# A hybrid decoder step on one core: the input stage asks for x earlier, holds three late weight slabs, and starts eight gathers of cached indexer keys

## The reference

```python
mod = (jax.nn.silu(c) @ w_ada + b_ada)[:, None, :]            # 6 x 1024 columns: shift, scale, gate, twice
h   = rms_norm(xp, g_attn_norm[l]) * (1 + ca_p) + sa_p        # 1024 prompt rows and 8 sample rows
p   = h @ w_in                                                # 1024 x 2536, split among the head groups
keys_idx = jnp.concatenate([past_rows(cache_idx, pages), ki]) # per request: 64 pages of 128 cached keys
r     = relu(einsum('qhd,sd->qhs', q_idx, keys_idx) * IDX_DIM ** -0.5)
score = einsum('qh,qhs->qs', w_idx, r)                        # its 256 largest choose the keys of sparse attention
```

## Time and profile before

| | us |
|---|---|
| median of 3 runs (lowest to highest) | 2939.24 (2938.51 to 2941.61) |
| the profiled execution | 2946.87 |
| its span, first to last instruction | 2945.1 |
| PE busy in the span | 2564.5 (87%) |
| DVE, ACT, POOL busy | 1515.4, 1103.8, 373.3 |
| DMA, mean over the span | 174 GB/s |

### The profile page before, as it was taken

One profiled execution on the slowest core, in us unless ns is written; L12 is line 12 of the kernel. 1 busy time (PEld: TensorE's weight loads), 2 busy tenths in 40 slices (PEclk: granted clock), 3 DMA queues, 4 the chain that ended last, 5 costly groups with the idle time before them and its releaser, 6 DMA issues. The chain is left out here.

```text
span 2945.1 us, 44078 instructions
## 1 busy us (share of the span) xinstructions
PE 2564.5 (87%) x14550; PEld 1470.6 (50%) x14550; DVE 1515.4 (51%) x3765; ACT 1103.8 (37%) x2376; POOL 373.3 (13%) x419
## 2 busy tenths in 40 slices
PE   4998996859989899895889969798999899999977
PEld 1443443538778687784566624344333333333332
DVE  1456544468878877784898664584111111111126
ACT  1223212449879578783655501221111111111110
POOL 0000001011011010101232131052000010000025
PEclk7999997969999899996999989898999999999988
DMA  8022158332145021206110084216989898897867
GB/s 326 17 83 84 36 177 290 142 105 72 54 151 207 5 104 36 86 6 175 36 34 18 9 272 128 101 36 238 398 315 396 327 346 327 321 372 274 317 249 276
DMA packets 252353, 511.70 MB, mean 174 GB/s; under 512 B 24138, under 2 KB 102156, under 8 KB 244761
## 3 DMA queue, kind: packets, MB, share of 16 engines
q1 hardware_dynamic: 196300, 311.88, 30.7%
q0 software_dynamic: 28640, 127.09, 11.7%
q10 hardware_dynamic: 27252, 70.69, 6.3%
HBM read 631.86 MB, written 86.93 MB: 244 GB/s over the span
## 5 line engine op out<-in xcount | busy, mean ns | idle before, releaser
L2906 PE MATMUL routed_ex_pG<-dispatch_exWG,routed_ex_XT 128*64 128x512 f32 x2048 | 459.9, 605 | 32.8 <-DMA dispatch_exWG<-in_w_e_gu 27.8
L2030 DVE TENSOR_REDUCE ssqc<-SQ 128x8 f32<-128x512 f32 x516 | 346.2, 683 | 127.1 <-ACT SQ L1833 113.6
L1744 PE MATMUL eK<-dWkv,LT 128*128 128x256 f32 x1032 | 318.8, 392 | 12.2 <-ACT SQ L1833 11.7
L1747 PE MATMUL eK<-WA,LT 128*128 128x272 f32 x1032 | 329.3, 401 | 0.0
L2906 PEld LDWEIGHTS routed_ex_pG<-dispatch_exWG,routed_ex_XT 128*64 128x64 f32 x2048 | 149.1, 140 | 338.1 <-issue 337.8
L1833 ACT ACTIVATE SQ<-eK 128x512 f32<-128x512 f32 x516 | 291.9, 602 | 59.1 <-PE eK L1747 43.5
L2997 DVE TENSOR_TENSOR routed_ex_sg<-routed_ex_sg,routed_ex_pG 128x256 f32<-128x256 f32 x64 | 27.0, 421 | 555.3 <-ACT routed_ex_sg L2954 555.3
L556 PE MATMUL in_pp<-ada_Win,in_hT 128*128 128x512 f32 (+1 forms) x640 | 280.9, 597 | 9.8 <-ACT in_pr L454 9.8
L2925 PE MATMUL routed_ex_pY<-routed_ex_WD,routed_ex_AT 128*64 128x512 f32 x1024 | 233.8, 598 | 0.9 <-DMA routed_ex_WD<-in_w_e_down 0.9
L1747 PEld LDWEIGHTS eK<-WA,LT 128*128 128x128 f32 x1032 | 202.1, 196 | 29.5 <-DVE numc L2029 0.2
L1744 PEld LDWEIGHTS eK<-dWkv,LT 128*128 128x128 f32 x1032 | 191.2, 197 | 48.2 <-ACT SQ L1833 16.9
(11 more groups left out here) (550 smaller groups left out, 3715.2 us busy)
## 6 DMA issues: line engine op xcount, KB each, us to landing
dispatch_exWG<-in_w_e_gu SPq DMA_DIRECT2D x256, 1024.0 KB
routed_ex_WD<-in_w_e_down SPq DMA_DIRECT2D x132, 1024.0 KB, 19.2
s_yblk<-routed_ex_Y ACTq DMA_DIRECT2D x64, 512.0 KB
ada_Win<-in_w_ada ACTq DMA_DIRECT2D x8, 2048.0 KB, 11.1
s_yblk<-zrows SPq DMA_DIRECT2D x15, 1024.0 KB
ada_Wada<-in_w_ada SPq DMA_DIRECT2D x8, 1024.0 KB, 16.2
ada_Win<-in_w_in ACTq DMA_DIRECT2D x4, 2048.0 KB, 11.5
dispatch_exWG<-in_w_e_gu SPq DMA_DIRECT2D x4, 2048.0 KB
```

The costliest lines, as they stand in the source:

```text
L1744: pe.matmul(pK[kn % 3][:, 512 + z:512 + z + HK], key, Wkv[:, 4:8, 0:NOPE], start=True, stop=True)
L1747: pe.matmul(pK[kn % 3][:, z:z + HK + 16], key, WA[:, pr, :], start=True, stop=True).then_inc(s_KN, 1)
L2030: dve.tensor_reduce(ssqc[cg % 2][:, n - 1 - tau, :], SQ[kn % 4].rearrange("p (h d) -> p h d", h=H), AX.X, ALU.add).then_inc(s_red, 1)
L2906: m = pe.matmul(pG[u][r, :], XT[u][:, k, r], WG[2 * u + v][:, k, :], start=(k == 0), stop=(k == KD - 1))
```

## The change

Five edits:

1. SP asks for x0 after four of the eight slabs in `stage_ada`, not after all eight.
2. The page table is read at the start of `stage_in`, behind the second tile of x, and DVE makes the row numbers in step 1 there. `stage_index` no longer does either.
3. ACT asks for late slab 1 together with slab 2, one `take` later, and first waits until the stores of tile 6 have landed. Slab 7 is asked for after the last tile's second-last group of `roots`, not with slabs 4 to 6. PE multiplies three slabs in step 8 and five in step 9, where it was four and four.
4. POOL gathers the first eight blocks of keys within `stage_in`, once `s_lm` says that all eight slabs have been multiplied, into columns 0 to 2047 of `Win`. Blocks 4 to 7 each wait until the block four before has landed. `Win` is kept until `stage_index` ends and takes the place of the `KI` buffers.
5. In `stage_index` PE transposes the first block before it turns the queries. The modulation's sum is written to `sq` instead of `pr`.

```diff
+NQI, NKI = 4, 8
+def cached_keys(T):
+    return T["cache_idx_k"][0].rearrange("n (j s) d -> (n j) (s d)", j=NQI)
+def key_slab(G, k):
+    return G["Win"][:, k, 0:32 * IDX]
@@ stage_ada, SP
             for k in range(KD):
+                if k == 4:
+                    sp.dma_start(G["x0"][:, :], T["x_prompt"][0, 0:P, :]).then_inc(G["s_x0"], 16)
                 sp.dma_start(W[k][:, :], T["w_ada"][0, k * P:(k + 1) * P, 0:2048]).then_inc(s_w[k], 16)
...
-            sp.dma_start(G["x0"][:, :], T["x_prompt"][0, 0:P, :]).then_inc(G["s_x0"], 16)
@@ stage_in, SP
             load(1)
+            sp.dma_start(G["pages"][:, :], T["page_table"].rearrange("(a b) p -> (b p) a", b=2), allow_slow_non_contiguous=True).then_inc(s_pg, 16)
...
-                    sp.dma_start(T["mod"][:, a:a + 512], pr[(NTT - 3) % 3][32 * j:32 * j + NC9, late(2 + b)]).then_inc(G["s_tail"], 16)
+                    sp.dma_start(T["mod"][:, a:a + 512], sq[32 * j:32 * j + NC9, late(b)]).then_inc(G["s_tail"], 16)
+        @block.gpsimd
+        def _(pool):
+            pool.wait_ge(s_idx, 1)
+            pool.wait_ge(s_lm, KD)
+            for g in range(NKI):
+                if g >= 4:
+                    pool.wait_ge(G["s_ki"][g - 4], 16)
+                pool.indirect_dma_start(out=key_slab(G, g), out_offset=None, in_=cached_keys(T),
+                                        in_offset=bass.IndirectOffsetOnAxis(ap=G["didx"][:, g // NQI, g % NQI:g % NQI + 1], axis=0)).then_inc(G["s_ki"][g], 16)
@@ stage_in, ACT
                 elif step == NTT:
-                    for k in range(4, KD):
+                    for k in range(4, KD - 1):
                         act.wait_ge(s_lm, k - 3)
                         late_weights(k)
...
                 take(step, 1)
-                if step == NTT - 1:
-                    late_weights(1)
...
                     roots(t, (4, 5))
+                    if t == NTT - 1:
+                        act.wait_ge(s_lm, 4)
+                        late_weights(KD - 1)
                 take(step, 2)
                 if step == NTT - 1:
+                    act.wait_ge(s_rd, NTT - 2)
+                    late_weights(1)
                     late_weights(2)
@@ stage_in, PE
                 if step == NTT - 1:
-                    for k in range(4):
+                    for k in range(3):
                         late_modulation(k)
                 elif step == NTT:
-                    for k in range(4, KD):
+                    for k in range(3, KD):
                         late_modulation(k)
@@ stage_in, DVE
+                if step == 1:
+                    dve.wait_ge(s_pg, 16)
+                    link(dve.tensor_copy(G["pagef"][:, :], G["pages"][:, :]))
...
+                    dve.sem_inc(s_idx, 1)
@@ stage_index, POOL
-            pool.wait_ge(s_idx, 1)
-            for g in range(NG):
-                if g >= NKI:
-                    pool.wait_ge(s_T, 4 * (g - NKI + 1))
-                if g >= 4:
-                    pool.wait_ge(s_k[(g - 4) % NKI], 16 * ((g - 4) // NKI + 1))
...
+            for g in range(NKI, NG):
+                pool.wait_ge(s_T, 4 * (g - NKI + 1))
+                pool.wait_ge(s_k[(g - 4) % NKI], 16 * ((g - 4) // NKI + 1))
...
@@ stage_index, PE
             turns(0)
+            queries()
             pe.wait_ge(s_qb, 1)
```

More of the change, by code:

```diff
@@ L171, in build @@
         G["pagef"] = sb("pagef", [P, NS // 2])
+        G["didx"] = sb("didx", [P, NS // 2, NQI], I32)
         G["SD"] = sb("SD", [P, NS // 2, PAGE + 1])
@@ L182, in build @@
                 G["s_tail"] = nc.alloc_semaphore("in_last_stores")
+                G["s_ki"] = [nc.alloc_semaphore(f"keys{i}") for i in range(NKI)]
                 G["s_win"] = [nc.alloc_semaphore(f"win{g}") for g in range(len(in_cols()))]
@@ L348, in stage_in @@
     late = lambda q: slice(512 * q, 512 * q + 512)
+    s_pg, s_idx = sem("in_pages"), sem("in_key_rows")
+    idxf = sb("idxf", [P, NS // 2, NQI])
     NROOT = 7
@@ L741, in _ @@
             for b in range(2):
[L742 to L743 removed]
+                dve.tensor_tensor(sq[:, late(b)], pp[b][:, :], pr[(NTT - 3) % 3][:, late(b)], ALU.add).then_inc(s_lmod, 1)
 def stage_prompt(nc, T, G, sem, sb, ps):
@@ L1319, in stage_index @@
     c, pages, pagef, SD = G["c"], G["pages"], G["pagef"], G["SD"]
-    NP2, NQ, NKI = NS // 2, 4, 8
+    NP2, NQ = NS // 2, NQI
     NG = NP2 * NQ
-    KI = [sb(f"KI{i}", [P, 32, IDX]) for i in range(NKI)]
+    KI = [key_slab(G, i).rearrange("p (s d) -> p s d", d=IDX) for i in range(NKI)]
     qr = sb("dqr", [NS, H, 2, IDX])
@@ L1332, in stage_index @@
     RL = [sb(f"RL{i}", [P, 512]) for i in range(2)]
-    idx, idxf = sb("didx", [P, NP2, NQ], I32), sb("didxf", [P, NP2, NQ])
+    idx = G["didx"]
     pT, pS, pZ = [ps(f"dT{i}") for i in range(4)], [ps("dS0"), ps("dS1")], [ps("dZ0"), ps("dZ1")]
-    s_pg, s_q, s_idx, s_qt, s_qb, s_T, s_evd, s_eva, s_S, s_R, s_v, s_z, s_wx, s_wc, s_ws, s_sd = (
-        sem("di_" + n) for n in ("pg", "q", "idx", "qt", "qb", "T", "evd", "eva", "S", "R", "v", "z", "wx", "wc", "ws", "sd"))
-    s_k = [sem(f"di_k{i}") for i in range(NKI)]
-    idx_rows = T["cache_idx_k"][0].rearrange("n (j s) d -> (n j) (s d)", j=NQ)
+    s_q, s_qt, s_qb, s_T, s_evd, s_eva, s_S, s_R, s_v, s_z, s_wx, s_wc, s_ws, s_sd = (
+        sem("di_" + n) for n in ("q", "qt", "qb", "T", "evd", "eva", "S", "R", "v", "z", "wx", "wc", "ws", "sd"))
+    s_k = G["s_ki"]
     fresh = T["o11"].rearrange("l b s d -> (l b s) d")
@@ L1352, in _ @@
         def _(pool):
-            pool.wait_ge(s_idx, 1)
-            for g in range(NG):
-                if g >= NKI:
-                    pool.wait_ge(s_T, 4 * (g - NKI + 1))
-                if g >= 4:
-                    pool.wait_ge(s_k[(g - 4) % NKI], 16 * ((g - 4) // NKI + 1))
-                pool.indirect_dma_start(out=KI[g % NKI][:, :, :].rearrange("p s d -> p (s d)"), out_offset=None, in_=idx_rows,
+            for g in range(NKI, NG):
+                pool.wait_ge(s_T, 4 * (g - NKI + 1))
+                pool.wait_ge(s_k[(g - 4) % NKI], 16 * ((g - 4) // NKI + 1))
+                pool.indirect_dma_start(out=key_slab(G, g % NKI), out_offset=None, in_=cached_keys(T),
                                         in_offset=bass.IndirectOffsetOnAxis(ap=idx[:, g // NQ, g % NQ:g % NQ + 1], axis=0)).then_inc(s_k[g % NKI], 16)
@@ L1363, in _, with queries @@
         def _(pe):
-            pe.wait_ge(s_q, 64)
-            for h in range(H):
-                m = pe.transpose(pZ[0][:, h * NS:(h + 1) * NS], qr[:, h, :, :].rearrange("b a d -> b (a d)"), c("ident")[0:NS, 0:NS])
-            m.then_inc(s_qt, 1)
-            pe.wait_ge(s_wx, 1)
-            pe.matmul(pZ[1][:, 0:NP2], WX[:, :, :].rearrange("b r h -> b (r h)"), c("pair_of")[0:NS, :], start=True, stop=True)
-            pe.matmul(pZ[1][:, NP2:2 * NP2], c("last_of")[0:NS, :], fpr[:, :], start=True, stop=True).then_inc(s_wc, 1)
+            def queries():
+                pe.wait_ge(s_q, 64)
+                for h in range(H):
+                    m = pe.transpose(pZ[0][:, h * NS:(h + 1) * NS], qr[:, h, :, :].rearrange("b a d -> b (a d)"), c("ident")[0:NS, 0:NS])
+                m.then_inc(s_qt, 1)
+                pe.wait_ge(s_wx, 1)
+                pe.matmul(pZ[1][:, 0:NP2], WX[:, :, :].rearrange("b r h -> b (r h)"), c("pair_of")[0:NS, :], start=True, stop=True)
+                pe.matmul(pZ[1][:, NP2:2 * NP2], c("last_of")[0:NS, :], fpr[:, :], start=True, stop=True).then_inc(s_wc, 1)
             def turns(g):
```

14 lines of the change are left out of this document (4 added, 10 removed).

## The result

| | before | after |
|---|---|---|
| median, us (lowest to highest, 5 runs each) | 2941.61 (2938.51 to 2944.34) | 2959.20 (2957.11 to 2966.79) |
| ratio, 95% interval | | 1.0069 (1.0052 to 1.0085) |
| the profiled execution, us | 2946.87 | 2958.91 |
| SP's first request of the index stage, us | 490.02 | 508.90 |
| PE's first product there, us | 504.72 | 520.99 |

What follows compares the result with a forecast made beforehand. It took DMA to bound the input loading, then a chain from ACT's slab requests through PE to SP's stores; PE bounds the index loop. 0 + 0 + 16.8 - 1.8 = 15.0 us on the median 2939.24 gave 2954.2, range 2940 to 2959.

Steps and rivals of the forecast that it cites:

- Edit 1, 0: Start of the input stage: asking for x0 earlier costs 0, as DMA engines are full and bytes the same.
- Edit 2, 0: Input stage: the early page table and row numbers cost 0, 1 us at most if the third tile is delayed.
- Edit 3, slabs: Input stage's end: ACT free 4.7 us sooner, slab 7 landed at 471.9, PE at the last tile 1.7 us later.
- Edit 4, gathers: Input stage's end: SP's stores move 52 pieces a microsecond under gathers; with the slabs, the stage ends 16.8 us later.
- Edit 5, -1.8: Index stage: first product 12.9 us after its start instead of 14.7, a gain of 1.8 us, bounds 1 and 3.4.
- Fair share: Rival, input stage's end: SP's stores get their fair share beside the gathers, total 2939.8 to 2944.7 us; chance 0.21.
- The slabs pay: Rival, input stage's end: the slabs pay and the gathers are hidden, faster, 2933.9 us; chance 0.07.
- More than forecast: Rival: stores slow the gathers, or queries land 3 us or more late behind queued stores, 2959 to 2965 us; chance 0.08.

Runs made afterwards that it cites:

- x0_only: Kernel before with edit 1 alone (x0 asked for after four slabs instead of eight); ratio to before 1.0008 (0.9998 to 1.0019).
- numbers_ready: Kernel before with edit 2, all gathers at the index stage's start, PE's order as before; ratio to before 0.9999 (0.9990 to 1.0008).
- slabs_only: Kernel before with edit 3 alone (three late slabs, then five, slab 7 asked for later); ratio to before 1.0005 (0.9996 to 1.0014).
- keys_first: numbers_ready with one difference: PE transposes the first keys ahead of the queries; ratio to before 1.0013 (1.0003 to 1.0024).
- x0_undone: Kernel after without edit 1 (x0 again asked for behind all eight slabs); ratio to before 1.0059 (1.0046 to 1.0073).
- gathers_held: Kernel after with POOL's eight early gathers held until SP has issued its last input-stage request; ratio to before 1.0109 (1.0093 to 1.0125).
- loads_ahead: Kernel before with page table and small loads asked for before the last tile's stores, s_mod before transposed stores, gathers at index stage's start; ratio 0.9986 (0.9976 to 0.9995).
- mods_first: Kernel after with SP's eight s_mod requests ahead of the last tile's transposed stores; ratio to before 1.0062 (1.0049 to 1.0075).
- gathers_only: Kernel after without edits 1 and 3, eight gathers still in the input stage; ratio to before 1.0050 (1.0035 to 1.0066).
- two_early: Kernel before with edit 2 and PE's new order, two gathers in the input stage, the rest in the index stage; ratio 1.0008 (0.9999 to 1.0017).
- mods_pages: mods_ahead with the page table read behind the last tile's plain stores and gathers at the index stage's start; ratio to before 1.0011 (1.0002 to 1.0021).
- mods_pages_act: mods_pages with the four loads of queries, wi and fresh key asked for by ACT instead of SP; ratio to before 1.0007 (0.9996 to 1.0018).
- mods_ahead: Kernel before with the eight s_mod stores asked for ahead of the last tile's transposed stores; ratio to before 0.9996 (0.9987 to 1.0005).

## Why the prediction was right or wrong

The direction and the main mechanism were right: slower, by stores that stand behind gathers. What failed are the two terms that I had put at nothing, edits 1 and 2. The time was 5.0 us too low (2959.2 against 2954.2), just above the stated range. 2.4 of these are the base, 2941.61 with two more runs instead of 2939.24. 1.3 are in the trace up to the first product (16.3 against 15.0) and the last 1.3 between the trace and the medians. Up to the last stage's barrier the trace is 17.1 us later, close to the medians' 17.6.

The start of the index stage came 18.9 us later, not 16.8. These 2.1 are a sum of misses with both signs: edit 1 +1.0, edit 2 +1.8, the slabs +0.4 (1.6 against 1.2), the gathers -1.2 (14.4 against the 15.6 that are left of 16.8 without the slabs' 1.2). That the forecast came near is in part luck: the gathers' term and edit 5 took back 2.0 of what the others had missed. By its steps:

- *Edit 1, 0: wrong, the step that failed in kind.* "The DMA engines are full and the bytes are the same" left out the time between ACT's request and its data. 2.5 us ran at 249 GB/s instead of 391. DVE starts 1.66 us later in after and 1.3 in x0_only; 1.0 is left at the index stage there. I had even named the price, 1.3 us, and called it covered.
- *Edit 2, 0: wrong.* In numbers_ready all of edit 2 and the new place of the sum stand at +1.8 where the index stage starts. 1.4 of it come back in the other kernels that have them, 0.4 of it at 182 us and 1.0 in SP's last requests; the page table's pieces ahead of the third tile, the one cost that I had looked at, is neither. Which of the moved things makes the 1.4 is open.
- *Edit 3, slabs: right in kind, mis-sized.* ACT was forecast free 4.7 us sooner; it was 3.8 in slabs_only and 2.5 in after. Slab 7 was forecast landed at 471.9; PE got it at 474.57 (473.64 in slabs_only), outside my 470 to 473. The "about 1 to be reported" in that sum was my guess, and no run shows it: from q10's last piece to PE's matmul it was 0.5 us, 474.1 to 474.57 in after and 467.0 to 467.47 in before. The wait of 8 us was 7.32, the sixteen matmuls 3.55 against 3.8. So PE reached the last tile at 478.05, not 475.7. At the full clock it won 0.86 back in its first eight transposes and 1.4 in all, where I had put 0.5, and SP asked at 483.59, not 482.1.
- *Edit 4, gathers: right, a little too large.* 53 pieces a microsecond against 52. They started 3.4 us later than forecast (479.09), for slab 7 and 1.0 us between PE's last matmul and POOL. POOL asked until 494.96, not 491. The two long requests waited 8.83 and, in the first `s_mod`, 10.50 us, 19.3 together (15 to 20 forecast). That `s_mod` was taken at 504.63, when 1916 of SP's pieces had moved since the request for `qmT`; I had counted on the 2285 of before. SP ended at 507.41 against 505.4. What I had missed is POOL's drain. It was hidden in after, and so my reading that "POOL's program ends at about 491" set a bound was 14 us off: it ended at 505.2.
- *Edit 5, -1.8: right, a little small.* 2.6 measured. The value hangs on the keys being there; without them the same order costs 4.5 us (keys_first).
- *Rivals.* Fair share is refuted by q1's 9.0%. "The slabs pay" asked for slab 7 within 5.4 us of its request; it took 10. "More than forecast" named 2959 to 2965, and the median lies at its lower edge, but not by its mechanism: the queries landed 2.5 us after the request (508.90 to 511.39), so nothing queued there, and the gathers were through near 503 us, no later against the forecast's 499.7 than they had started. The drain that waits for the gathers stood in no rival; the later runs brought it out.

Open: edit 1's exact share within the whole change (in x0_undone the clock's jump took it back), what makes edit 2's 1.4 us, and why the last stage of the program differs by some us between executions.

## What to carry to other kernels

Before a bulk transfer is moved into an idle stretch, look for what small-piece traffic runs there and who waits for its requests: here a queue of 512-byte stores beside 8 KB gathers got one piece for one, 53 a microsecond. A gather of POOL also belonged to the block in which it was asked for: the drain at the barrier lasted until its data had moved (10.2 us in gathers_held). What paid (0.9986 in loads_ahead) was the reverse of the change: the small requests first, in gaps of SP's queue, and the bulk transfer behind the barrier; and when the last queue before a handover is shortened, look for what bridges the time until the next queue's data flows: here nothing did, and 2.5 us ran at 249 GB/s instead of 391.

## What the hardware showed that I had not expected

- POOL's drain at a barrier waits for its gathers: 11.4 us in after, 11.5 in x0_undone, 11.0 in mods_first, 11.6 in gathers_only and 10.2 in gathers_held with eight, 9.6 in two_early with two, each ending within a microsecond or so of the last piece. Without a gather it took 0.03 us.
- A request of ACT brings its first pieces late: in after, asked for at 26.49 us, the first moved after 27.5, and 72 pieces had moved by 29, where the same queue moved 192 in one microsecond later on (471 to 472 us). With no other queue to bridge this, the DMA engines ran for 2.5 us at 249 GB/s instead of 391.
- Four tiny loads took 10.8 us from request to use beside gathers and stores (mods_pages), 8.9 by another queue (mods_pages_act), 4.0 beside the stores alone (mods_ahead), 2.8 with neither (before).
- Within 318 to 323 us the granted clock came back from 0.50 to 1.00 later in the profiles of four kernels (0.59 to 0.65 in that window against 0.90 in before and 0.82 in numbers_ready, whose input stage does the same work as that of keys_first, one of the four), which put everything behind it 1.5 to 1.6 us later.
